# Identity products on TensorE in nine pauses, and modulation ahead of a weight tile's split at three norms

## The reference, cut to what matters

```python
for layer in range(DEPTH):
    hp = modulate(rmsnorm(xp, norm1_g[layer]), p_sh1, p_sc1)
    hs = modulate(rmsnorm(xs, norm1_g[layer]), s_sh1, s_sc1)
    ...                                    # mixer (layer 0) or attention (layer 1): yp, ys
    xp, xs = xp + p_g1 * yp, xs + s_g1 * ys
    hp = modulate(rmsnorm(xp, norm2_g[layer]), p_sh2, p_sc2)
    hs = modulate(rmsnorm(xs, norm2_g[layer]), s_sh2, s_sc2)
    ...                                    # SwiGLU (layer 0) or experts (layer 1): fp, fs
    xp, xs = xp + p_g2 * fp, xs + s_g2 * fs

def moe_swiglu(x, w_router, b_router, w1, w3, w2):
    logits = xt @ w_router + b_router
    top_v, top_i = lax.top_k(logits, TOP_K)
    gates = jnp.sum(one_hot(top_i, N_EXPERTS) * softmax(top_v)[..., None], axis=1)
    for e in range(N_EXPERTS):
        out = out + gates[:, e:e + 1] * swiglu(xt, w1[e], w3[e], w2[e])
```

## Time and profile before

| | |
|---|---|
| time, median of 3 runs | 1497.81 us (1497.46 to 1505.38) |
| the profiled execution's own time | 1496.2 us |
| its span, first to last instruction | 1494.4 us |
| mean granted TensorE clock | 0.956 |
| TensorE busy | 1366.9 us, 91% |
| VectorE busy | 1045.6 us, 70% |
| ScalarE busy | 818.4 us, 55% |

### The profile page before, as it was taken

One profiled execution on the slowest core, in us unless ns is written; L12 is line 12 of the kernel. 1 busy time (PEld: TensorE's weight loads), 2 busy tenths in 40 slices (PEclk: granted clock), 3 DMA queues, 4 the chain that ended last, 5 costly groups with the idle time before them and its releaser, 6 DMA issues.

```text
span 1494.4 us, 16388 instructions
## 1 busy us (share of the span) xinstructions
PE 1366.9 (91%) x6400; PEld 1070.9 (72%) x6400; DVE 1045.6 (70%) x1015; ACT 818.4 (55%) x908; POOL 25.4 (2%) x44
## 2 busy tenths in 40 slices
PE   4879899679999897778999999999999999999994
PEld 1555465468888676767888888878888888888783
DVE  0454345564454566456889889898898998988985
ACT  1432221344434455445777776777777777777672
POOL 3000000000000010000000000000000000000000
PEclk9899989799999998989999999999999999999997
DMA  9887775835556450244999999999999999999990
GB/s 329 286 280 248 265 278 196 243 113 169 180 187 196 141 157 4 85 169 142 341 364 352 354 337 351 362 360 353 332 349 363 361 354 340 346 349 368 352 343 30
DMA packets 288116, 400.94 MB, mean 268 GB/s; under 512 B 15973, under 2 KB 224064, under 8 KB 287968
## 3 DMA queue, kind: packets, MB, share of 16 engines
q1 hardware_dynamic: 282048, 391.23, 77.5%
q0 software_dynamic: 1792, 4.28, 0.9%
q10 hardware_dynamic: 4192, 4.31, 0.9%
HBM read 397.93 MB, written 1.84 MB: 268 GB/s over the span
## 4 chain that ended last, share of the span: by engine, by line
PE 79%; DVE 3%; ACT 2%; issue 1%; DMA 1%; DVEq 0%; SPq 0%; ACTq 0%
PE bank L1759 77%; PE bank L2130 2%; DMA raw<-in_ev_w_out 1%; ACT arena L1028 1%; PE bank L1810 0%; ACT xn L777 0%; ACT w_hi L494 0%; PE bank L2229 0%; ACT arena L1038 0%; ACT Gb L796 0%; DVE arena L1749 0%; DVE arena L1523 0%; DVE x L1524 0%; DVE x L1750 0%; DVE Gb L1199 0%
## 5 line engine op out<-in xcount | busy, mean ns | idle before, releaser
L501 DVE TENSOR_TENSOR w_lo<-raw,w_hi 128x2048 fp32r<-128x2048 f32 (+1 forms) x238 | 543.3, 2283 | 165.2 <-ACT w_hi L494 163.5
L494 ACT CAST w_hi<-raw 128x2048 fp32r<-128x2048 f32 (+1 forms) x238 | 451.7, 1898 | 173.6 <-PE bank L1759 94.0
L1759 PE MATMUL bank<-w_hi,x_hi 128*128 128x512 f32 x1072 | 438.2, 409 | 29.7 <-issue 15.9
L1759 PE MATMUL bank<-w_lo,x_hi 128*128 128x512 f32 x1072 | 426.4, 398 | 0.0
L1759 PE MATMUL bank<-w_hi,x_lo 128*128 128x512 f32 x1072 | 423.5, 395 | 0.0
L1759 PEld LDWEIGHTS bank<-w_hi,x_hi 128*128 128x128 f32 x1072 | 204.5, 191 | 79.0 <-issue 32.1
L1759 PEld LDWEIGHTS bank<-w_hi,x_lo 128*128 128x128 f32 x1072 | 204.6, 191 | 47.3
L1759 PEld LDWEIGHTS bank<-w_lo,x_hi 128*128 128x128 f32 x1072 | 205.2, 191 | 39.4 <-issue 0.2
L501 DVE TENSOR_TENSOR w_lo<-arena,w_hi 128x2048 fp32r<-128x2048 f32 x88 | 201.7, 2292 | 36.9 <-ACT w_hi L494 36.7
L494 ACT CAST w_hi<-arena 128x2048 fp32r<-128x2048 f32 x88 | 168.0, 1909 | 27.8 <-PE bank L1759 27.8
L1759 PE MATMUL bank<-w_hi,g_hi 128*128 128x512 f32 x440 | 174.0, 395 | 1.8 <-DVE g_lo L1480 1.8
(11 more groups left out here) (279 smaller groups left out, 940.8 us busy)
## 6 DMA issues: line engine op xcount, KB each, us to landing
raw<-in_moe_w SPq DMA_DIRECT2D x352, 512.0 KB, 5.6
arena<-in_moe_w SPq DMA_DIRECT2D x176, 512.0 KB, 5.6
raw<-in_w_ada SPq DMA_DIRECT2D x96, 512.0 KB, 7.0
raw<-in_ff_w SPq DMA_DIRECT2D x66, 512.0 KB, 4.5
raw<-in_ev_w_in SPq DMA_DIRECT2D x28, 512.0 KB, 7.0
raw<-in_at_w_qkv SPq DMA_DIRECT2D x12, 512.0 KB, 4.6
raw<-in_ev_w_out SPq DMA_DIRECT2D x8, 512.0 KB, 16.3
raw<-in_at_w_out SPq DMA_DIRECT2D x8, 512.0 KB, 4.4
```

Source lines behind the costliest of these rows:

```text
L494: nc.scalar.copy(w_hi[:, t % SPL, c], place[:, c]).then_inc(hi_ok, 1)
L501: nc.vector.tensor_tensor(w_lo[:, t % SPL, c], raw_slot(n)[0][:, c], w_hi[:, t % SPL, c].bitcast(F32), ALU.subtract).then_inc(lo_ok, 1)
L1759: return pe.matmul(out, lhsT, rhs, start=start, stop=stop)
```

## The change

There are two parts. A new function `idle_products(b, n)` multiplies `ident_r` by itself, repeated four times over 512 columns, n times into PSUM bank b; nothing reads the result, and the bank is free and written afresh afterwards. It is called at nine places, with 101 products in all. And at norms 1, 2 and 3 `take_turned` now stands ahead of the weight tile's split, on ScalarE and on VectorE.

```diff
# ScalarE
             norm_root(1)
+            take_turned(2, 2)
             high(FF0 + 2)
-            take_turned(2, 2)
...
             norm_root(2)
+            take_turned(3, 1)
             high(QKV0 + 2)
-            take_turned(3, 1)
...
             norm_root(3)
+            take_turned(5, 3)
             high(MOE0 + 2)
-            take_turned(5, 3)
# VectorE
             norm_rows(1)
+            take_turned(2, 2)
             low(FF0 + 2)
-            take_turned(2, 2)
...
             norm_rows(2)
+            take_turned(3, 1)
             low(QKV0 + 1)
-            take_turned(3, 1)
             low(QKV0 + 2)
...
             norm_rows(3)
+            take_turned(5, 3)
             low(MOE0 + 2)
-            take_turned(5, 3)
# TensorE
+            def idle_products(b, n):
+
+                for _i in range(n):
+                    mm(bank[b][:, :], ident_r[:], ident_r[:].unsqueeze(1).to_broadcast([P, 4, P]), True, True)
...
+            eng.wait_ge(gbt, 4)
+            idle_products(7, 14)
             turn_rows(2)
             eng.wait_ge(ro_t, 4)
+            idle_products(0, 8)
             for c in range(NCH):
                 wide(FFN0, c, 0)
...
+            idle_products(3, 17)
             turn_rows(3)
+            idle_products(3, 6)
...
+            idle_products(6, 15)
             turn_queries(0)
...
                 if v + 1 < KV:
                     scores(v + 1)
                 b = 3 * (v % 2)
+                if v == 0:
+                    idle_products(7, 10)
                 eng.wait_ge(sc_e, v + 1)
...
+            idle_products(7, 14)
             turn_rows(5)
             eng.wait_ge(hT_a, 8)
             eng.wait_ge(hT_d, 8)
             eng.wait_ge(ro_t, 8)
             eng.wait_ge(ld_r, 32)
+            idle_products(2, 7)
             for g in range(G):
...
             mm(bank[1][:, 16:24], ones[:, :], sel[:, 1, :], False, True).then_inc(r_pos, 1)
+            idle_products(0, 10)
```

## The result

The changed kernel takes **1483.88 us** in the median of 4 runs (1480.69 to 1484.04). The kernel before, run beside it, takes 1500.97 (1497.46 to 1505.38). The ratio is 0.9883, with a 95% interval of 0.9841 to 0.9926: faster, by between 11 and 24 us. The prediction of 1481.0, between 1475 and 1491, holds, and so does its sign. The two profiled executions differ by less: spans of 1494.4 and 1482.0 us, 12.4 apart. With the runs of all experiments taken together the gain is nearer to the ledger than to these medians: 50 runs of the kernel before have a mean of 1497.9 us, 8 of the change (these and experiment 5) one of 1484.0, 13.9 apart.

What follows compares the result with a forecast made beforehand. It took the experts' start behind the router as the bound, delayed by TensorE's pauses and the half clock behind them. Terms 3.9 + 3.0 + 5.0 + 4.9 = 16.8 us off the 1497.8 median gave 1481.0, range 1475 to 1491.

Steps and rivals of the forecast that it cites:

- Norm 1: At norm 1, 2.4 us from the earlier modulation and 1.4 to 1.5 from products at full clock: 3.9 us gained.
- Norm 2: At norm 2, 1.4 us from the order and 1.6 from eight products no longer at half clock: 3.0 us gained.
- The narrow cover of 0.5 us: At norm 2, the second weight tile's low part ends near 532.4 us and is wanted at 532.9.
- Attention: Values, scores and turning at full clock give 6.8 us, less 1.8 for one fall: 5.0, between 2 and 6.8.
- I count on one such fall among these five places: In attention's unfilled pauses, the clock falls to half once, costing 1.8 us.
- Norm 3, router, gather: From norm 3 to the gather, order 2.4, fillers -1.6, router 2.8, gather 2.5, less 1.2: 4.9, between 1 and 6.3.
- The 1.2 for one fall: In the router's part, one half-clock stretch expected among thin eight-column products, costing 1.2 us.
- The sum: The four terms together: 16.8 us gained, or 19.8 with no fall of the clock at all.
- Heads only: Rival: the clock holds at norms 1 and 2 but falls in attention and router; 1486 to 1491 us, chance 0.15.
- Transposes don't count: Rival: the sixteen transposes let the clock fall, so later fillers and first products run slow; 1487.5 us, chance 0.04.
- The identity doesn't count: Rival: identity products move almost only zeros, the clock falls as before, only order remains; 1498 to 1501, chance 0.07.
- Fillers overrun: Rival: fillers take 0.42 us each from their first product and outlast their pauses; 1510 us, slower, chance 0.04.

Runs made afterwards that it cites:

- experiment 5: The changed kernel run again, not altered, for a second profile: 1485.0 us, ratio 0.991 to the kernel before.
- Experiment 1: The changed kernel without any identity products, keeping only the moved order at the norms: 1490.27 us, ratio 0.9944 to the kernel before.
- experiment 2: The changed kernel with all 101 products but the six moved calls back in their old places: 1493.29 us, ratio 0.9971 to the kernel before.
- experiment 9: The changed kernel without the 7 products ahead of the router: 1481.28 us, ratio 0.9888 to the kernel before.
- 3 to 6: The first two are the changed kernel without attention's 25 products, run twice: 1485.36 and 1482.93 us. Experiment 5 and experiment 6 have their own lines.
- experiment 6: The changed kernel with products also in the pauses inside the attention loop: 1478.4 us, ratio 0.9869 to the kernel before.
- experiment 11: The changed kernel with 34 instead of 17 products ahead of norm 2's transposes: 1483.42 us, ratio 0.9934 to the kernel before.
- kernels 8 to 10: The first is the changed kernel with the router's 7 products put as 9 behind norm 3's transposes: 1484.33 us. Experiment 9 and experiment 10 have their own lines.
- experiment 10: The changed kernel with the attention loop filled, 9 products behind norm 3's transposes and 10 ahead of the output projection: 1474.74 us, ratio 0.9842 to the kernel before.

## Why the prediction was right, and where it was wrong

**Norm 1: 3.9 predicted, 3.79 measured.** Order 2.4, measured 2.28; clock 1.4 to 1.5, measured 1.51. The first real product comes 4.95 us behind the first transpose instead of 7.24. But the prediction priced the two as if they were independent, and experiments 1 and 2 show that they aren't: the order without fillers gives 1.8, since the transposes stay cold, and the fillers without the order give neither start nor clock.

**Norm 2: 3.0 predicted, 2.97 measured** (2.0 in the change's second profile, by VectorE's slower rows). Order 1.34 of 1.4, clock 1.63 of 1.6. The narrow cover of 0.5 us over the second weight tile held: TensorE shows no pause in the projection's first rounds.

**Attention: 5.0 predicted, between 2 and 6.8; measured a loss of 0.64, and in the second profile a gain of 1.2.** This term failed. The step was "I count on one such fall among these five places". In the profiled execution there were four in the loop, and one more at the rows' transposes. Before, cold groups cost 7.0 us by the prediction's sum; after, they cost 1.6 + 1.6 + 2.5 for two scores and the last values, and some 0.7 for the second scores (from their start to the first values 9.2 us, and 8.5 in the filled loop). That is 6.4, in keeping with a stretch shorter by 0.36. Entering the output projection cold costs 1.0 more. The evidence for the forecast was that the loop before had run warm from 607.56 on; that was one draw, and it was read as a property of the code. The price of a cold group was right; their number was not.

The deeper error is one of cause. The 25 products at the head leave the loop's own pauses as they were, and no gain from them shows: means of 56.0 and 56.1 us. The pauses left open, 2.6 us behind the first scores and 0.7 to 0.9 on either side of the values, are what lets the clock fall: filled, 51.0 in three of three kernels. The prediction named both. The first, cold second scores and ten fillers that end up to 1.1 us late, it took as one possible fall among five; it came in all six kernels and cost 0.9 to 2.2 us up to the turned probabilities. The cold scores and values in the rounds behind vary among these six, from none in experiment 9 to three in the change. Which of the loop's short pauses weighs most was not separated. Without the 5.0 of this term the sum is 11.8, near the 12.4 between the spans.

**Norm 3, router, gather: 4.9 predicted, between 1 and 6.3; measured 5.92.** Move less fillers 0.59 against 0.8, the router 3.20 against 2.8, the gather 2.13 against 2.5. The 1.2 for one fall did not come due in this execution. Of the six traces with the same code from norm 3 to the experts (the change, 3 to 6 and 11) five take 23.8 us from first transpose to experts, and the sixth 25.4 (5), where the last fillers were cold and overran. So the allowance was larger than its mean, some 0.3 us. The cold routers of 5.25, 4.80 and 4.32 us belong to kernels 8 to 10, in which the seven fillers stand elsewhere or are gone. On the router alone the seven don't pay: with them it ends 0.5 us later behind the first transpose than without (9). What puts the kernel with them 1.25 us ahead in that comparison is that its last ten fillers were warm, and experiment 5 shows that the seven don't ensure this.

**The sum** was 16.8, the spans give 12.4, and 5.6 of shortfall in attention is the difference, less 1.0 more at the router and 0.4 outside the change (16.8 - 12.4 = 4.4; 5.6 + 0.2 at the norms - 1.0 - 0.4). The medians differ by 17.1. That this is so near to 16.8 is luck: an attention term wrong by 5.6 us was made up by four runs of the kernel before with a median of 1500.97, where all 50 have a mean of 1497.9. Against that the gain is 13.9 us, 3 below the forecast, and the range holds the time of 1484 with or without the luck. Runs of the kernel before lie between 1491 and 1506 us in all comparisons. What causes that spread wasn't settled; the stretch ahead of norm 1, which only experiment 10 touches, ended between 310.0 and 318.2 us in these traces, and the clock's place in the mixer is an explanation that I haven't tested.

**The rivals.** Heads only: true in attention, where its 0 to 3 was closest, false at the router; by its own account 1486 to 1491, which is not what came. Transposes don't count: refuted. Products behind the sixteen transposes were warm at norms 1 and 2, and in experiment 6 the clock read 1.00 over 20 us of attention with its transposes in it. The Trainium skill's "TensorE: Matmul & The Clock Gate", Part 4, says that they don't engage the full clock. The row that the prediction set against it, sixteen transposes at 1.00, shows only that the clock did not fall within 2 us of them. Experiment 1 is better evidence: behind sixteen transposes and nothing else since a pause of 4.0 us, the products of norm 1 ran 0.23 us apart. No run here agrees with the Trainium skill on this point, though none has transposes alone over a long stretch. The identity doesn't count: refuted, since fillers alone keep the clock through 4 us of pause, and 34 in a row kept it for 8. Fillers overrun: not by being cold ahead of the norms' transposes and the turned queries, where all were warm from their first product. But it is real where a filling follows work that may have run cold: the last ten, behind the thin products, were cold themselves in 5, 9 and 10, and the ten ahead of the first turned probabilities were warm but late behind cold second scores. The same page of the Trainium skill, Part 1, says that the gate isn't aligned to the kernel's start and that the number of slow products varies between runs. The runs agree: the same program had different groups cold in its two profiles (5), and the prediction gave this too little weight.

## What to carry to other kernels

Look at what the engine waits for behind a filling before you fill: here fillings with 0.65 to 1.0 us of pause behind them held the clock and those with 2.4 to 2.9 before the next stream did not (one of 2.35 did, in six traces, so these numbers are no limit), and the chain had to be shortened for the filling to pay. Fill all the pauses of a loop, also those of 0.7 us, and not just the long one ahead of it; and keep fillings out of places where the work ahead may itself have run cold, since a filling that is cold or starts late overruns. When groups are cold at some places of one trace, look at a second execution before you price any of them.

## What was not expected of the hardware

- A product of the identity with itself, nearly all zeros, holds the clock at 1.00 (8 us of them in experiment 11), and costs 0.23 us for 512 columns warm and 0.44 cold (ten in 2.5 and 4.6 us).
- TensorE can lose its full clock while it is busy, on thin products: the router's 32 records of 8 columns took 5.25 us though a filling ended 0.26 us ahead of them, against 3.63; the granted clock reads 1.00 at their start and 0.50 at their end.
- A pause of 2.35 us behind norm 3's transposes did not make the seven products behind it cold (1.70 us for seven) in any of six traces, while one of 2.94 at norm 1 in experiment 2 made the SwiGLU's first products cold.
- Where the clock falls is not a property of the code alone: 51.87 to 57.49 us for the same attention code in six kernels, and 50.95 to 50.97 in three once its pauses were filled.
